# Samples' attention scores over cached keys as TensorE products on transposed keys, and the attention loop moved up behind the top-k with eleven feature tiles in it

## The chip, the cores and the metric

The kernel runs on one core of a Trainium2 chip. The metric is the device time of one execution in microseconds (us). A core has a matrix engine (TensorE, "PE" in the profile, with its weight loads as "PEld"), a vector engine (VectorE, "DVE"), a scalar engine (ScalarE, "ACT"), a general engine (GpSimd, "POOL") and a queue processor (SyncE, "SP"). Each engine works through its own list of instructions in order; they meet only at semaphores.

## What the reference computes

Two decoder layers for one prompt of 512 tokens and eight samples (one new token each). The part that the change touches is the sparse attention of the samples: index scores over 256 cached keys and the new one, the best 64 of them, and softmax attention over those.

```python
def select_keys(qi, wi, ki, qpos, topk):
    s = jnp.einsum('bqhd,bsd->bqhs', qi.astype(jnp.float32), ki.astype(jnp.float32)) * IDX_DIM ** -0.5
    score = jnp.einsum('bqhs,bqh->bqs', jax.nn.relu(s), wi.astype(jnp.float32) * N_IDX_HEADS ** -0.5)
    ...
    _, idx = lax.top_k(score, topk)
...
def dsa_sample(q, k, v, qi, ki, wi, ck, cv, cki, page_table):
    ...
    ki_all = jnp.concatenate([cki[page_table].reshape(n_dec, past, IDX_DIM), ki], axis=1)
    topk = min(TOPK_MAX, (past + t_dec) // 4)
    ...
    return attend(q, kg, vg, valid).reshape(n_dec, t_dec, A_W)
```

There are 4 heads of 64 channels, 8 index heads of 32 channels, and 2 cached pages of 128 keys for each sample. In every layer three other token mixers (a short gated convolution, a convolution of width 31, a state-space scan) and the gated feed-forward part stand beside this.

## The kernel before, in words

A layer is one block of code per engine, run twice by a loop over the layers. All activations are kept with channels on partitions and the 520 tokens (512 of the prompt, 8 of the samples) along the free side.

The stage that matters here runs as follows in each layer.

1. Token products (PE L678 to L697) give queries, keys, values and index queries, with tokens on partitions.
2. DVE adds up the prompt's index scores and takes the best 128 keys of each query in 16 rounds of MAX8 and MATCH_REPLACE (L1550, L1554), then turns the marks into masks (L1558).
3. Under these rounds PE works on *feature tiles*: 18 tiles of 128 output channels, each 48 products (L724). A weight tile is loaded by SP, its upper part cast by ACT (`tile_upper`, L1135), its lower part subtracted by POOL (`tile_lower`, L2034). When a tile's last product is done, ACT first casts the weights of the tile after next and then copies the tile out of PSUM (L1189, inside `feature_out`).
4. After the rounds DVE works out the samples' scores (`for b in range(NS)`, L1567 to L1580): PE spreads a sample's query over all partitions (`spread`, L737 and L738), and DVE multiplies the cached keys by it and adds up over the channels. Between two spreads PE does half a feature tile; four tiles lie there.
5. Then the *attention loop*: 16 steps (`STEPS`: four query blocks by four heads). In step j, PE makes logits (L863), DVE adds the mask and takes the maximum (L1800, L1803), ACT takes the exponential (L1268), DVE divides (L1813), PE transposes the probabilities (L904), ACT copies them out (L1280), and PE mixes the values (L893). PE does `step_products(j)` feature products ahead of the transposes and as many behind them. DVE has one other task in each step (the samples' top-k, softplus, the short convolutions, the samples' states). Five feature tiles lie in the loop.
6. Tiles up to number `LOOP_TILES` alternate between two pairs of PSUM banks; those after it use banks 0 and 1 alone:

```python
        def tile_bank(i):

            return 2 * (i % 2) if i <= LOOP_TILES else 0
...
                                if i >= 2:
                                    pe.wait_ge(feat_ready, i - 1 if i <= LOOP_TILES + 1 else i)
```

so that within the loop a tile's first product waits until ACT has copied the tile before it.

7. Behind the loop PE's first work is `cumulate(0)` (L927), the start of the scan of the prompt.

## Time and profile before

| what | value |
|---|---|
| median of 3 runs | 1547.42 us (1546.89 to 1548.22) |
| profiled execution, its own time | 1550.66 us |
| its span, first to last instruction | 1549.1 us |
| time around the span | 1.56 us |
| mean granted PE clock | 0.96 of full |
| PE busy | 1424.0 us (92%) |
| DVE busy | 844.8 us (55%) |
| ACT busy | 537.3 us (35%) |
| POOL busy | 203.1 us (13%) |

The shares are means over the whole program. The two layers run the same code, one after the other; the first layer's attention stage lies between about 100 and 277 us of the span, and the second layer's is the same some 762 us later. The views by stretch, by engine in order of time and by waits tell what holds this stage up.

### The profile page before, as it was taken

What the parts mean: (1) busy time and instruction counts of PE and PEld (TensorE: products, weight loads), DVE (VectorE), ACT (ScalarE), POOL (GpSimd) and SP (SyncE); (2) the same over time, 40 slices, a digit from 0 to 9 for tenths busy, and PEclk for the clock granted to TensorE, in tenths of its full rate; (3) what the DMA queues carried; (4) which work ended last, traced back from release to release, by engine and by line L of the source; (5) the groups of instructions that cost most, each with busy time, mean ns of one, the idle gap of its engine ahead of it and who ended that gap; (6) DMA issues with size and microseconds to landing.
All of it is one profiled execution on the core that took longest, in us unless ns stands there. A gap on an engine that the chain in (4) does not pass through costs nothing. (4 is left out here: it accounts for less than half of the span.)

```text
span 1549.1 us, 28682 instructions
## 1 busy us (share of the span) xinstructions
PE 1424.0 (92%) x11510; PEld 1319.7 (85%) x11510; DVE 844.8 (55%) x1729; ACT 537.3 (35%) x879; POOL 203.1 (13%) x138
## 2 busy tenths in 40 slices
PE   4999878997999999999769998799989999999995
PEld 4889864897999999999657997558979999999994
DVE  5489998735444444222446898976264443442224
ACT  3443234444322222222344422445342232222222
POOL 1334312020000000000040442311200000000010
PEclk8999988999999999999879998999999999999997
DMA  6443231221333332233055333212313233323221
GB/s 222 133 133 96 80 85 44 97 86 44 94 94 95 88 88 83 76 93 93 9 201 146 104 87 88 81 40 87 96 55 95 84 92 95 92 64 94 84 73 55
DMA packets 222718, 141.20 MB, mean 91 GB/s; under 512 B 13514, under 2 KB 218674, under 8 KB 222102
## 3 DMA queue, kind: packets, MB, share of 16 engines
q1 hardware_dynamic: 220006, 132.57, 29.0%
q0 software_dynamic: 2624, 7.48, 1.3%
q8 instruction: 53, 0.87, 0.2%
q14 instruction: 35, 0.29, 0.1%
HBM read 124.66 MB, written 11.77 MB: 88 GB/s over the span
## 5 line engine op out<-in xcount | busy, mean ns | idle before, releaser
L1861 DVE TENSOR_TENSOR w_lo<-ring,w_hi 128x1024 fp32r<-128x1024 f32 (+2 forms) x164 | 179.3, 1093 | 399.2 <-ACT w_hi L1247 399.2
L623 PE MATMUL PS<-u_hi,w_hi 128*128 128x260 f32 x1600 | 325.5, 285 | 15.4 <-DVE u_lo L1982 11.7
L1247 ACT CAST w_hi<-ring 128x1024 fp32r<-128x1024 f32 (+2 forms) x168 | 158.9, 946 | 473.3 <-PE PS L623 473.3
L623 PE MATMUL PS<-u_hi,w_lo 128*128 128x260 f32 x1600 | 322.4, 283 | 0.0
L623 PE MATMUL PS<-u_lo,w_hi 128*128 128x260 f32 x1408 | 283.8, 283 | 0.0
L623 PEld LDWEIGHTS PS<-u_hi,w_hi 128*128 128x128 f32 x1600 | 246.8, 189 | 18.8 <-issue 13.0
L623 PEld LDWEIGHTS PS<-u_hi,w_lo 128*128 128x128 f32 x1600 | 247.4, 189 | 0.0
L623 PEld LDWEIGHTS PS<-u_lo,w_hi 128*128 128x128 f32 x1408 | 218.3, 189 | 0.0
L623 PE MATMUL PS<-hid_hi,w_hi 128*128 128x260 f32 x704 | 141.8, 283 | 3.6 <-ACTq L1404 3.6
L623 PE MATMUL PS<-hid_hi,w_lo 128*128 128x260 f32 x704 | 141.8, 283 | 0.0
L623 PE MATMUL PS<-hid_lo,w_hi 128*128 128x260 f32 x704 | 141.4, 282 | 0.0
L724 PE MATMUL PS<-u_hi,w_hi 128*128 128x260 f32 x576 | 123.2, 295 | 14.1 <-ACT hid L1189 14.1
L724 PE MATMUL PS<-m_lo,w_hi 128*128 128x260 f32 x576 | 121.7, 291 | 0.0
L2034 POOL TENSOR_TENSOR w_lo<-ring,w_hi 128x1024 fp32r<-128x1024 f32 x36 | 86.3, 2397 | 270.5 <-ACT w_hi L1135 270.4
L724 PE MATMUL PS<-u_hi,w_lo 128*128 128x260 f32 x576 | 121.4, 292 | 0.0
L2115 POOL TENSOR_TENSOR side<-side 128x520 f32<-128x520 f32 x12 | 15.7, 1307 | 762.0 <-ACT u L1415 762.0
L623 PEld LDWEIGHTS PS<-hid_hi,w_hi 128*128 128x128 f32 x704 | 108.4, 188 | 3.9 <-issue 3.9
L724 PEld LDWEIGHTS PS<-u_hi,w_hi 128*128 128x128 f32 x576 | 92.1, 195 | 21.0 <-ACT hid L1189 15.6
L623 PEld LDWEIGHTS PS<-hid_hi,w_lo 128*128 128x128 f32 x704 | 108.4, 188 | 0.0
L623 PEld LDWEIGHTS PS<-hid_lo,w_hi 128*128 128x128 f32 x704 | 108.4, 188 | 0.0
L1999 DVE TENSOR_TENSOR side<-m_lo,PS 128x520 f32<-128x520 f32 x44 | 30.7, 697 | 120.5 <-PE PS L623 120.5
L724 PEld LDWEIGHTS PS<-m_lo,w_hi 128*128 128x128 f32 x576 | 92.3, 194 | 3.2 <-issue 3.2
(346 smaller groups left out, 2192.2 us busy)
## 6 DMA issues: line engine op xcount, KB each, us to landing
ring<-in_ffn_gate SPq DMA_DIRECT2D x44, 512.0 KB, 3.7
ring<-in_ffn_up SPq DMA_DIRECT2D x44, 512.0 KB, 3.7
ring<-in_w_in SPq DMA_DIRECT2D x36, 512.0 KB, 3.6
ring<-in_ffn_down SPq DMA_DIRECT2D x32, 384.0 KB, 3.4
ring<-in_ffn_down SPq DMA_DIRECT2D x32, 320.0 KB, 3.0
ring<-in_w_out SPq DMA_DIRECT2D x16, 512.0 KB, 4.1
x_store<-x SPq DMA_DIRECT2D x2, 2080.0 KB, 15.4
x<-x_store SPq DMA_DIRECT2D x2, 2080.0 KB, 7.8
```

What stands on the lines that cost most here:

```text
L623: ins = pe.matmul(to[:, h, :], w[:, k - base, :], a[k][:, h * HALF:(h + 1) * HALF], start=(begin and w is whi and a is a_hi), stop=(end an ...
L724: last = pe.matmul(bank(tile_bank(i) + h)[:, 0:HALF], w[i % 2][:, k, :], t[:, h * HALF:(h + 1) * HALF], start=(k == 0 and a == 0), stop=(k ...
L1247: act.copy(w_hi[part % 2][:, 0:n, :], raw[part % 4][:, 0:n, :]).then_inc(part_hi, 1)
L1861: dve.tensor_tensor(w_lo[part % 2][:, 0:n, :], raw[part % 4][:, 0:n, :], w_hi[part % 2][:, 0:n, :].bitcast(F32), ALU.subtract).then_inc(pa ...
L1999: dve.tensor_tensor(halves(hid_f[:, c, :]), halves(rstd_all), pair(2 * c + 1), ALU.mult).then_inc(factors_ready, 1)
L2034: pool.tensor_tensor(w_lo[f % 2][:, :, :], raw[(f + 2) % 4], w_hi[f % 2][:, :, :].bitcast(F32), ALU.subtract).then_inc(tile_lo, 1)
L2115: pool.tensor_tensor(squares[:, 0, :], squares[:, 0, :], squares[:, m, :], ALU.add).then_inc(added, 1)
```

## The change

The samples' scores are no longer made by DVE. PE transposes the index keys and the keys of the cache into PSUM (`keys_prepare`, `keys_turn`), ACT copies them to SBUF, and PE multiplies them by the samples' queries, laid out as columns (`index_logits`, `key_products`, `index_scores`). DVE keeps three small preparations (`keys_prepared`, in round 10 of the top-k) and one copy. The attention loop follows the top-k at once. It now has 16 feature products in each half of each of the 16 steps, eleven tiles in all; only five tiles and a third lie ahead of it. The order of the feature slabs is another one, the side tasks of DVE stand in other steps, the samples' states begin in step 11 in place of 13 and use banks 2 and 3, and the convolution of width 31 on PE stands in steps 15 to 17.

The numbers that set the order:

```diff
 
 
-        FEAT_SLABS = [5, 4, 3, 6, 7, 8, 2, 0, 1]
+        FEAT_SLABS = [4, 6, 7, 8, 3, 2, 0, 5, 1]
         N_TOK = 3
 
...
-        SPREAD_FROM = 7
         PER_TILE = 6 * KC
-        PER_SPREAD = PER_TILE // 2
+        PER_PART = PER_TILE // 3
         TAIL_TILES = 2
-        STEP_PRODUCTS = (14, 12, 13, 9, 13, 9, 13, 9, 13, 9, 9)
-        LOOP_TILES = SPREAD_FROM + NS * PER_SPREAD // PER_TILE
-        DENSE_STEPS = 11
+        LOOP_TILES = 5
+        LOOP_FIRST = LOOP_TILES * PER_TILE + PER_PART
         TAIL_PRODUCTS = (8, 20, 20, 12, 36)
         LAST_TILE = len(FEAT_SLABS) * 2 - TAIL_TILES
-        STATES_FROM = 13
+        STATES_FROM = 11
         FIRST_FFN = [(q, [k]) for k in range(5) for q in range(3)] + [(0, [5, 6, 7]), (2, [5, 6, 7]), (1, [5, 6, 7])]
-        TAP_SETS = {12: 2, 13: 3, 14: 3, 15: 3, 16: 3, 17: 2}
+        TAP_SETS = {15: 4, 16: 4, 17: 8}
```

The new functions on PE, and where they stand:

```diff
+                    def keys_prepare():
+
+                        pe.wait_ge(turned_ready, 7)
+                        pe.wait_ge(rope_done, 5)
+                        pe.wait_ge(ki_cache_in, 16 * 2 * NS)
+                        for t in range(NS // 2):
+                            last = pe.transpose(bank(4)[:, t * P:(t + 1) * P],
+                                                ki_cache[:, 4 * t:4 * t + 4, :].rearrange("p i c -> p (i c)"), ident)
+                        last.then_inc(key_pe, 1)
+                        for c in range(2):
+                            pe.transpose(bank(5)[:, c * NS:(c + 1) * NS], tok8[:, c * P:(c + 1) * P], ident[0:NS, 0:NS])
+                            pe.transpose(bank(5)[:, 16 + c * NS:16 + (c + 1) * NS], tok8[:, 3 * W + c * P:3 * W + (c + 1) * P],
+                                         ident[0:NS, 0:NS])
+                        for g in range(4):
+                            last = pe.matmul(bank(5)[32 * g:32 * g + IH, 32:32 + NS], tok8[:, TOK_W - IH:TOK_W], ident[0:NS, 0:NS],
+                                             start=True, stop=True)
+                        last.then_inc(key_prep, 1)
...
+                    def keys_turn(b):
+
+                        if b == 0:
...
+                            pe.wait_ge(keys_kept, b)
+                        for c in range(2):
+                            for pg in range(2):
+                                last = pe.transpose(bank(6 + b % 2)[:, c * W + pg * P:c * W + (pg + 1) * P],
+                                                    k_cache[:, 2 * b + pg, c * P:(c + 1) * P], ident)
+                        last.then_inc(key_pe, 1)
...
+                    def index_logits():
+
+                        pe.wait_ge(queries_kept, 1)
+                        pe.wait_ge(keys_kept, 1 + NS)
+                        for q in range(2):
...
+                        last.then_inc(key_logits, 1)
+
+                    def key_products(q):
+
+                        pe.wait_ge(keys_kept, 1 + 4 * (q + 1))
+                        for c in range(2):
+                            for g in range(4):
+                                b = 4 * q + g
+                                last = pe.matmul(bank(4)[32 * g:32 * g + HEADS, q * W:(q + 1) * W], q_cols[:, c, b, :],
+                                                 k_turned_of[b][:, c * W:(c + 1) * W], start=(c == 0), stop=(c == 1))
+                        if q:
+                            last.then_inc(key_logits, 1)
...
+                    def index_scores():
+
+                        pe.wait_ge(logits_kept, 2)
+                        pe.wait_ge(keys_kept, 1 + NS)
+                        for q in range(2):
+                            last = pe.matmul(bank(6)[0:NS, 0:W], wi_cols[:, q, :], idx_part[:, q * W:(q + 1) * W],
+                                             start=(q == 0), stop=(q == 1))
+                        last.then_inc(dec_pe, 1)
...
-                    feature_products((SPREAD_FROM - 2) * PER_TILE)
-                    pe.wait_ge(turned_ready, 7)
-                    pe.wait_ge(rows_lo_ready, 2)
...
+                        if b in (0, 2, 4, 6):
+                            feature_products(PER_PART)
+                        keys_turn(b)
+                    index_queries()
+                    feature_products(PER_PART)
+                    index_logits()
+                    key_products(0)
+                    feature_products(PER_PART)
+                    key_products(1)
+                    feature_products(LOOP_FIRST - feat_i[0] - PER_PART)
+                    index_scores()
+                    feature_products(PER_PART)
...
+                    def decode_mask():
+
+                        pe.wait_ge(dec_dve, 2)
                         pe.wait_ge(feat_ready, LOOP_TILES + 1)
...
+                        for b in range(NS):
+                            q, r = b // 4, 32 * (b % 4)
+                            last = pe.matmul(bank(2 + q)[r:r + 32, 0:261], ident[0:NS, b:b + 1].broadcast_to([NS, 32]),
+                                             m_row[0:NS, :], start=True, stop=True)
                         last.then_inc(dec_pe, 1)
```

What ACT and DVE do for them, and what DVE no longer does:

```diff
+                    act.copy(ident_r[:, :], ident[0:NS, 0:NS]).then_inc(picks_ready, 1)
+                    act.wait_ge(key_pe, 1)
+                    act.copy(ki_turned, bank(4)).then_inc(keys_kept, 1)
+                    for b in range(NS):
+                        act.wait_ge(key_pe, b + 2)
+                        act.copy(k_turned_of[b], bank(6 + b % 2)).then_inc(keys_kept, 1)
+                        if b == 3:
+                            feature_out(3)
                     feature_out(4)
-                    act.wait_ge(rope_done, 5)
-                    act.copy(rows_hi[:, 0:W], tok8[:, 0:W]).then_inc(rows_hi_ready, 1)
-                    act.copy(rows_hi[:, W:SPREAD_W], tok8[:, 3 * W:TOK_W]).then_inc(rows_hi_ready, 1)
-                    act.copy(ident_r[:, :], ident[0:NS, 0:NS]).then_inc(rows_hi_ready, 1)
+                    act.wait_ge(key_prep, 2)
+                    act.copy(qi_cols.rearrange("p h b -> p (h b)"), bank(5)[:, 64:128]).then_inc(queries_kept, 1)
+                    act.wait_ge(key_logits, 1)
+                    for pg in range(2):
+                        act.activation(idx_part.rearrange("p (q g k) -> p q g k", q=2, g=2)[:, :, pg],
+                                       bank(5 + 2 * pg)[:, 0:W].rearrange("p (q k) -> p q k", q=2), ACT.Relu).then_inc(logits_kept, 1)
+                    act.wait_ge(key_logits, 2)
+                    act.activation(l_row[:, :, 0:W], bank(4).rearrange("p (q k) -> p q k", q=2), ACT.Copy, scale=const("row_used"))\
+                       .then_inc(logits_kept, 1)
                     feature_out(LOOP_TILES)
...
+                    def keys_prepared():
+
+                        dve.wait_ge(key_prep, 1)
+                        step(dve.tensor_tensor(q_cols, bank(5)[:, 0:16].rearrange("p (c b) -> p c b", c=2).unsqueeze(3)
...
+                        settle()
+                        dve.sem_inc(key_dve, 1)
...
-                    dve.wait_ge(k_cache_in, 16 * 2 * NS)
-                    dve.wait_ge(ki_cache_in, 16 * 2 * NS)
-                    for b in range(NS):
-                        qb, ib = bank(4 + 2 * (b % 2)), bank(5 + 2 * (b % 2))
-                        dve.wait_ge(rows_spread, b + 1)
-                        kb = k_cache[:, 2 * b:2 * b + 2, :]
-                        step(dve.tensor_tensor(kb, kb, qb[:, 0:W].unsqueeze(1).broadcast_to([P, 2, W]), ALU.mult))
-                        pi = prod_i.rearrange("p (g h c) -> p g h c", g=2, c=ID)
-                        for pg in range(2):
-                            step(dve.tensor_tensor(pi[:, pg], ki_cache[:, 2 * b + pg, :].unsqueeze(1).broadcast_to([P, IH, ID]),
-                                                   ib[:, 0:W].rearrange("p (h c) -> p h c", c=ID), ALU.mult))
-                        settle()
-                        step(dve.tensor_reduce(past_l[:, :, b, :], kb.rearrange("p g (h c) -> p g h c", c=HD), AX.X, ALU.add))
-                        s16 = sc64[:, 0:16].rearrange("p (g h) -> p g h", g=2)
-                        step(dve.tensor_reduce(s16, pi, AX.X, ALU.add))
-                        settle()
-                        dve.scalar_tensor_tensor(s16, s16, 0.0, ib[:, W + ID:W + ID + IH].unsqueeze(1).broadcast_to([P, 2, IH]),
-                                                 ALU.max, ALU.mult).then_inc(rows_used, 1)
-                        dve.wait_ge(rows_used, b + 1)
-                        step(dve.tensor_reduce(past_s[:, :, b], s16, AX.X, ALU.add))
+                    dve.wait_ge(dec_pe, 1)
+                    step(dve.tensor_copy(s_row[0:NS, 0:W], bank(6)[0:NS, 0:W]))
```

The order of PE's loop and DVE's side tasks:

```diff
-                    pe.wait_ge(rows_used, NS - 1)
+                    pe.wait_ge(logits_kept, 3)
...
+                        if j == 10:
                             turn_state_rows()
-                        if j == 12:
+                        if j == 16:
                             turn_tails()
...
-                        if j == 4:
+                        if j == 3:
                             decode_mask()
-                        if j == 7:
+                        if j == 6:
                             decode_prob_turn()
+                        if j == 8:
+                            decode_mix()
                         if j == 9:
-                            decode_mix()
-                        if j == 10:
                             decode_pick()
...
+                    pe.wait_ge(conv_c_done, 1)
                     cumulate(0)
...
-                            gate_c()
+                            dve.wait_ge(dec_dve, 1)
+                            decode_best(TOPK_SAMPLE // 16)
                         elif j == 2:
-                            decode_scores()
-                            decode_best(TOPK_SAMPLE // 16)
-                        elif j == 3:
                             decode_best(TOPK_SAMPLE // 16)
                             decode_mask()
+                        elif j == 3:
+                            softplus()
                         elif j == 4:
-                            softplus()
+                            decode_logits()
                         elif j == 5:
-                            decode_logits()
+                            decode_probs()
                             conv_d_samples()
...
+                            gate_c()
+                        elif j == 9:
                             conv_d(2)
-                        elif j == 9:
+                        elif j == 10:
+                            state_rows()
                             conv_d(3)
+                        if j == 15:
+                            conv_b(0)
+                        if STATES_FROM <= j < STATES_FROM + NS // 2:
+                            sample_states(j - STATES_FROM)
+                        if j == 11:
                             conv_d(4)
-                        elif j == 10:
+                        elif j == 12:
                             conv_d(5)
                             settle()
                             dve.sem_inc(conv_d_done, 1)
-                        elif j == 11:
-                            state_rows()
+                        elif j == 13:
                             gate_b()
-                        elif j == 12:
-                            conv_b(0)
-                        elif STATES_FROM <= j < STATES_FROM + NS // 2:
-                            sample_states(j - STATES_FROM)
```

TensorE ahead of the loop. In the order before, the last feature products of a tile (L724) are followed by the first sample's spread: the query (`rows_hi`, `rows_lo_q`) and the index query, then half a tile.

```order
L724 MATMUL PS<-u_hi,w_hi_86 128x260 x2
L724 MATMUL PS<-m_lo_70,w_hi_86 128x260 x2
L724 MATMUL PS<-u_hi,w_lo_88 128x260 x2
L737 MATMUL PS<-rows_hi,ident_r 128x256
L738 MATMUL PS<-rows_lo_q,ident_r 128x256
L737 MATMUL PS<-rows_hi,ident_r 128x296
L738 MATMUL PS<-rows_lo_i,ident_r 128x296
```

In the changed order the same place has the last two samples' key transposes (L761, reading `side`), the index queries (L749), a third of a tile (L721), the index logits (L774) and the first half of the key products (L785).

```order
L761 MATMUL PS<-cst,side 128x128 x8
L749 MATMUL PS<-arena,cst 32x64 x4
L721 MATMUL PS<-m_lo_68,w_hi_87 128x260 x2
L721 MATMUL PS<-u_hi,w_lo_89 128x260 x2
L721 MATMUL PS<-u_hi,w_hi_87 128x260 x2
L721 MATMUL PS<-m_lo_69,w_hi_87 128x260 x2
L721 MATMUL PS<-u_hi,w_lo_89 128x260 x2
L721 MATMUL PS<-u_hi,w_hi_87 128x260 x2
L721 MATMUL PS<-m_lo_70,w_hi_87 128x260 x2
L721 MATMUL PS<-u_hi,w_lo_89 128x260 x2
L774 MATMUL PS<-side 8x128 x16
L785 MATMUL PS<-side 4x256 x8
```

The eight spreads are gone; two groups of key work stand where one spread stood, and half tiles have become thirds.

VectorE behind the top-k. Before, the masks (L1558) are followed by a sample's six instructions, eight times over.

```order
L1558 TENSOR_SCALAR arena<-arena 128x512
L1567 TENSOR_TENSOR side<-side,PS 128x512
L1570 TENSOR_TENSOR side<-side,PS 128x256 x2
L1573 TENSOR_REDUCE side<-side 128x2x4
L1575 TENSOR_REDUCE side<-side 128x16
L1577 SCALAR_TENSOR_TENSOR side<-side,PS 128x16
L1580 TENSOR_REDUCE side<-side 128x2
```

Now one copy of eight rows (L1655) stands between the masks (L1651) and the loop's first instruction (L1872).

```order
L1651 TENSOR_SCALAR arena<-arena 128x512
L1655 COPY side<-PS 8x256
L1872 ISA arena,small<-PS,cst 128x128
L1872 ISA small 128x1
L1875 TENSOR_SCALAR small<-small 128x1
```

Forty-eight instructions have gone from this place on DVE.

ScalarE in the loop. Before, the first four exponentials (L1268) of 128 keys and the copies of the probabilities (L1280) have one weight cast (L1135) with its tile's copy (L1189) among them.

```order
L1280 COPY arena<-PS 128x128
L1135 CAST w_hi_87<-ring 128x1024
L1189 ACTIVATE hid<-PS 128x520
L1268 ACTIVATE arena,small<-arena,small 128x128
L1280 COPY arena<-PS 128x128
L1268 ACTIVATE arena,small<-arena,small 128x128
L1280 COPY arena<-PS 128x128
L1135 CAST w_hi_86<-ring 128x1024
L1189 ACTIVATE hid<-PS 128x520
```

Now a cast (L1196) and a tile's copy (L1250) come about every one and a half steps, between the same exponentials (L1344) and copies (L1359); L1284 is the samples' exponential.

```order
L1196 CAST w_hi_87<-ring 128x1024
L1250 ACTIVATE hid<-PS 128x520
L1344 ACTIVATE arena,small<-arena,small 128x256
L1359 COPY arena<-PS 128x128
L1284 ACTIVATE side<-side 128x257 x2
L1344 ACTIVATE arena,small<-arena,small 128x256
L1196 CAST w_hi_86<-ring 128x1024
L1250 ACTIVATE hid<-PS 128x520
L1359 COPY arena<-PS 128x256
```

The cast stands ahead of the copy in each pair, as before; there are eleven pairs in the loop in place of five.

## Rows read from the trace of the kernel before

**Rows 1.** Page: span, and each engine's busy time.

```profile
span 1549.1 us, 28682 instructions
PE 1424.0 (92%) x11510; PEld 1319.7 (85%) x11510; DVE 844.8 (55%) x1729; ACT 537.3 (35%) x879; POOL 203.1 (13%) x138
```

**Rows 2.** Waits, 176 to 276.5 us: who waited for whom; total, times, longest us.

```profile
PE PS L724 <- ACT hid L1189: 7.8, 3, 4.4
...
PE PS L834 <- DVE hid L1739: 3.4, 1, 3.4
...
PE PS L904 <- DVE arena L1813: 3.1, 3, 2.0
...
PE PS L759 <- ACT hid L1189: 1.3, 1, 1.3
...
PE PS L808 <- ACT hid L1189: 1.2, 1, 1.2
```

**Rows 3.** Timeline of PE, 63 to 277 us: start, duration, instructions, idle before.

```profile
63.39 0.71 PE L639 MATMUL PS<-arena 32*128 32x256 f32 x8
...
115.13 1.91 PE L646 MATMUL PS<-cst,arena 128*128 128x128 f32 x16
116.80 0.48 PE L724 MATMUL PS<-u_hi,w_hi 128*128 128x260 f32 x2
117.12 0.41 PE L724 MATMUL PS<-m_lo,w_hi 128*128 128x260 f32 x2
...
145.81 0.38 PE L737 MATMUL PS<-rows_hi,ident_r 8*128 8x256 f32 x1
...
149.58 0.38 PE L737 MATMUL PS<-rows_hi,ident_r 8*128 8x256 f32 x1
...
176.01 0.49 PE L863 MATMUL PS<-arena 64*128 64x128 f32 x4
...
212.26 0.80 PE L724 MATMUL PS<-u_hi,w_hi 128*128 128x260 f32 x2 [4.38 <-ACT hid L1189]
...
232.01 1.07 PE L787 MATMUL PS<-x,side 128*32 128x256 f32 x16
...
276.54 2.05 PE L927 MATMUL PS<-cst,dt_tiles 128*128 128x128 f32 x16
```

**Rows 4.** Timeline of DVE, 147 to 218 us.

```profile
147.31 2.93 DVE L1558 TENSOR_SCALAR arena<-arena 128x256 f32<-128x256 f32 x3
150.28 0.69 DVE L1567 TENSOR_TENSOR side<-side,PS 128x512 f32<-128x512 f32 x1
...
153.26 0.68 DVE L1567 TENSOR_TENSOR side<-side,PS 128x512 f32<-128x512 f32 x1
...
175.94 0.17 DVE L1580 TENSOR_REDUCE side<-side 128x2 f32<-128x16 f32 x1
...
211.78 4.50 DVE L1719 SCALAR_TENSOR_TENSOR side<-hid,par,side 128x511 f32<-128x511 f32 x3
...
217.76 2.32 DVE L1719 SCALAR_TENSOR_TENSOR side<-hid,par,side 128x511 f32<-128x511 f32 x3
```

**Rows 5.** Timeline of POOL, 211 to 247 us.

```profile
211.79 2.37 POOL L2034 TENSOR_TENSOR w_lo<-ring,w_hi 128x1024 fp32r<-128x1024 f32 x1 [10.76 <-ACT w_hi L1135]
...
242.55 3.65 POOL L2073 TENSOR_TENSOR side<-cst,tap_col 128x2048 f32<-128x2048 f32 x1
```

**Rows 6.** Timeline of ACT, 197 to 199 us.

```profile
197.51 1.05 ACT L1135 CAST w_hi<-ring 128x1024 fp32r<-128x1024 f32 x1 [3.18 <-PE PS L724]
198.46 0.60 ACT L1189 ACTIVATE hid<-PS 128x520 f32<-128x520 f32 x1
```

**Rows 7.** Stretches of 10 us: busy of PE, PEld, DVE, ACT, POOL; granted PE clock; DMA.

```profile
190.00:200.00 10.00, 6.29 (x36) 4.84 (x36) 9.35 (x35) 2.80 (x7) 1.36 (x1) 0.83 0.48 122
...
210.00:220.00 10.00, 7.74 (x45) 7.27 (x47) 9.61 (x19) 3.08 (x8) 2.37 (x1) 0.66 0.37 107
...
240.00:250.00 10.00, 6.56 (x36) 3.38 (x36) 9.68 (x20) 2.37 (x6) 6.17 (x4) 0.58 0.46 157
```

249 lines of the change are left out of this document (126 added, 123 removed).

## The prediction

> **What bounds the kernel now.** I read the page first. PE is busy for 92% of the span and DVE for 55% [rows 1], so over the whole program a shorter DVE list is worth nothing by itself; it counts only where PE waits for it. So next came the stage of the change. In the first layer the top-k ends at 150.24 (147.31 plus 2.93), the eight samples' scores run from 150.28 to 176.11, and the attention loop begins at once [rows 4]. PE's own list shows that it is not idle under these scores: it starts a sample's spread at 145.81 and 149.58, with half a feature tile between, and its first product of the loop stands at 176.01 [rows 3]. Both engines come to the loop at the same moment. Of the loop, from 176.01 to `cumulate(0)` at 276.54, the view of waits gives PE's idle time: 7.8 + 3.4 + 3.1 + 1.3 + 1.2 = 16.8 us [rows 2]. Only 3.1 us of it is the wait for probabilities from DVE. Most, 7.8 us, is PE waiting for ACT to empty the one PSUM pair (the largest 4.38 us at 212.26 [rows 3]). The stretches then show a second loss: the granted clock is 0.83, 0.66 and 0.58 in three slices of 10 us, each with PE under 8 us busy [rows 7]. Busy time times the missing clock is 6.29 x 0.17 + 7.74 x 0.34 + 6.56 x 0.42 = 6.5 us. So in each layer some 23 us of PE time between 115 and 277 could be had, and everything else there is PE's work. That is the ceiling of the gain, 2 x 23 = 46 us, not the 2 x 25.9 us that DVE loses.
>
> **The change part by part, for one layer.**
>
> *DVE's scores.* 150.28 to 176.11 is 25.8 us, 2.98 a sample (150.28 to 153.26 [rows 4]) plus small waits near the end. In their place stand three small preparations, about 0.8 us (I take the price of three small instructions of 0.17 us with their starts and the wait between them), and a copy of about 0.4. DVE therefore starts the loop at 150.2 + 1.2 = 151.5, or 25 us sooner. The cost of this to PE is nothing directly.
>
> *PE ahead of the loop.* The work removed is eight spreads. 145.81 to 149.58 is 3.77 us for one spread and 24 feature products. Five tiles, 240 products, take from 116.80 to 145.81, or 0.121 us each, so 24 cost 2.90 and a spread 0.87; eight are 7.0 us [rows 3]. Added are 36 transposes of 128x128; sixteen such took 115.13 to 116.80, 0.104 each, so 3.8 us [rows 3]. Eight tiny products and the four of the index queries I bound between 0 and 0.104 each and take 1.6 us with their starts. The sixteen index logits: four products of 256 columns in four row groups took 0.71 us [rows 3]; with half the columns, four groups of four are between 4 x 0.36 and half of that, so 1.0. The sixteen key products have the shape of the samples' mix (sixteen records, that is eight products, about 1.05 us [rows 3]), so 2.1. The two index scores are 0.9 (between the mix's pace, 0.3, and two logits, 1.1). Sum 9.4, net +2.4.
>
> *PE in the loop.* The mask is eight products for one (+0.5), the probabilities' turn six transposes for three small ones (+0.4), and the turn of the scores goes (-0.4). Feature products are cut into about nine more pieces; the first pair of a piece takes 0.32 us (116.80 to 117.12) where a pair costs 0.24 [rows 3], so +0.9 with rounding up. Work in sum: +2.4 + 0.5 + 0.9 = +3.8 us. Feature products themselves only move: 16 tiles before, 16 now.
>
> *When PE reaches the loop.* 116.80 + 160 products (19.3) + 9.4 + waits. ACT copies the transposed keys out under the feature products; only before the index logits must PE wait, for a weight cast, a tile's copy (0.95 + 0.60 [rows 6]) and the copy of the queries, 2.1 us in all. So PE is there at about 149, before DVE at 151.5. It fills the gap with the 48 products that stand ahead of its first wait (5.8 us).
>
> *The waits in the loop.* Eleven tiles in one PSUM pair make nine boundaries at which PE must wait for ACT. ACT casts first and copies then: 197.51 to 199.06 is 1.55 us, and with the product's own tail and the semaphores a bare boundary costs PE 1.9 [rows 6]. I walked the sixteen steps with each engine in its own order and prices as in these rows. The boundaries then cost 1.7, 0.9, 0.7, 1.2, 1.6, 1.8 (here it is the samples' output that is waited for), 0, 1.9 and 2.5: 12.3 us. Where the mask's products or transposes stand between two tiles, they hide a part of ACT's 1.55. The waits for probabilities come to 4.6, nearly all in steps 13 to 15, where DVE has two tasks in a step and ACT the SiLU of the convolution with its table loads. With 2.3 ahead of the loop this is 19.2 us, against 16.8 before: +2.4. The same walk in the order of before reaches `cumulate(0)` at 275.0, where the trace has 276.54; that is how far I trust it.
>
> *The clock.* With PE never idle for more than 2.5 us I expect less of the low clock, not none: the last steps look like 190 to 200 us of now [rows 7]. Of the 6.5 us I leave 2.8: -3.7. Both ends are possible, 0 and 6.5, and they enter the range.
>
> *DVE against POOL.* At 211.78 a group of three instructions took 4.50 us where the same group took 2.32 at 217.76; POOL lowered a weight tile from 211.79 on for 2.37 us [rows 4, 5]. Such a collision costs DVE up to 2.2 us. Under MAX8 and MATCH_REPLACE the lowerings cost it nothing. Now five more of them fall into the loop: +11 us for DVE. Its loop took 176.1 to about 276, so it would take at most 100 + 11 + 1 = 112 us, from 151.5 to 263.5. That is still ahead of PE, so the term is nothing on PE's path but the late waits counted above. The Trainium skill ("SBUF — State Buffer", Who interferes with whom) says that a DVE instruction with two SBUF inputs is fully blocked by a GpSimd one that reads SBUF; by it eleven lowerings of 2.37 and the tap weights' 3.65 [rows 5] could stop DVE for 29.7 us in place of the 15 or so of before, and its end would be near 267, the sum for PE unchanged.
>
> *Tail, loads.* Behind the loop PE's order is the same, and so are the products in it. The caches' rows are wanted some 30 us sooner than now, behind the first feature products, but their loads keep their place far ahead in the queues' lists, SP's weight loads keep their order, and POOL's state load now waits for the samples' mix in step 8 and is needed in step 11, some 18 us later. I cost these at nothing; if the state load were late, PE's spreads would stop in step 11.
>
> **Sum.** Work +3.8, waits +2.4, clock -3.7: +2.5 us a layer, +5 us for two. Against the profiled execution's own 1550.66 this is 1555.7; that execution was 3.2 us above the median, so against the median it is 1547.4 + 5 = 1552.
>
> **The rivals.**
>
> *A. The loop closes up (faster).* The ledger's waits are the soft term. If transposes and logits hide ACT's 1.55 us at most of the nine boundaries, as they do at the one that costs nothing, waits fall from 19.2 to 11, and with PE then hardly idle the clock stays at its full level: +3.8 - 5.8 - 6.5 = -8.5 a layer, 1530. For it speaks that DVE is 25 us ahead; against it, that ACT casts before it copies, and that five boundaries have the next tile's product almost directly behind. It decides from waits under 16.5 us a layer on with the clock as I have it. 0.27, for anything from 1525 to 1544.
>
> *B. The clock takes it back.* PE is now on the path at every moment, so a slice at 0.6 costs its full 4 us, where before it cost partly slack. If the three slices of [rows 7] come again, the clock term is 0: +6.2 a layer and 1560. For it: nine idle gaps of 1 to 2.5 us; against it, that the slices of now follow gaps of 3.4 and 4.4. 0.15.
>
> *C. DVE becomes the bound.* If collisions cost DVE the 29.7 us, it ends at 151.5 + 100 + 14.7 + 1 = 267, 10 us ahead of PE. Only if each of the sixteen steps adds a little over 1 us more in which DVE and PE wait for each other in turn, 18 us, does it end near 285; then the layer loses 8: 1547.4 + 16 = 1564. The price of DVE's list speaks against it; it decides from an end of DVE behind 277 on. 0.06.
>
> *D. My forecast, and around it no effect:* what DVE gives up was hidden behind PE. 0.52, and in this case 1546 to 1558.
>
> **Chances and range.** A measurement of this kernel tells about 0.2% (3.1 us) from no change, so faster means below 1544.3 and slower above 1550.5. Case A gives 0.25 faster and 0.02 same. Case D gives 0.23 same, 0.27 slower and 0.02 faster. B and C are slower, 0.21. Faster 0.27, same 0.25, slower 0.48. The work term is open by 2 us a layer, the waits by 3 in either direction, the clock from -2.8 to +3.7; taken together that is 5.5 a layer or 11 in all: 1541 to 1563. For eight in ten this leaves out most of A below 1541 and a little of C.
>
> **What the profile after would show.** L1872 first at about 151.5, PE's first logits near 149, `cumulate(0)` between 276 and 281 in the first layer. PE's waits in the loop are mostly for ACT's tile copy, some nine of 1 to 2 us; DVE idle for some 35 us of the loop. The clock is below 0.9 in one slice rather than three. The prediction is wrong if `cumulate(0)` stands before 273, which would mean that the boundaries were hidden, or after 283; and wrong in its reason if the largest wait of PE in the loop is for DVE.

## The result, and the profile after

| | changed kernel | before |
|---|---|---|
| median of 20 runs | 1550.6 us (1548.58 to 1555.91) | 1548.94 us (1545.3 to 1552.29) |
| ratio | 1.0018, interval 1.0009 to 1.0026 | |
| profiled execution, its own time | 1550.77 us | 1550.66 us |

The change costs 1.4 to 4.0 us by this interval, most likely 2.8; a later measurement of the same two kernels gave 1.0017 (1.0006 to 1.0027). The forecast was 4.6 us above the median of before, with 1541 to 1563 as its range. In the two profiled executions the difference is 0.1 us, so the traces don't show the 2.8 us as one place. They show how the parts of the sum came out.

About half of the cost sits in a few executions. Of the 32 executions of the changed kernel in the two measurements, nine took 1553.84 to 1555.91 us, longer than any of the 102 of the kernel before that are on record beside these runs (1552.75 at most); the other 23 average 1550.3 us. The mean granted clock of the nine is 0.959, that of the 23 is 0.962; this is worth some 4 us of PE's 1428, most of the 4.7 by which they are longer. Neither trace of the changed kernel (1550.77 and 1550.88 us) is of one of the nine, so what lowers the clock in them stays open.

The page of the changed kernel, against [rows 1]: DVE has lost 50.8 us of work and PE has gained 3.5.

```profile
span 1549.2 us, 29026 instructions
PE 1427.5 (92%) x11720; PEld 1325.7 (86%) x11720; DVE 794.0 (51%) x1623; ACT 550.9 (36%) x907; POOL 200.9 (13%) x134
```

The timeline of PE in the first layer, against [rows 3]: start, duration, instructions, idle before.

```profile
118.67 0.66 PE L733 MATMUL PS<-cst,side 128*128 128x128 f32 x4
...
119.75 0.51 PE L721 MATMUL PS<-u_hi,w_lo 128*128 128x260 f32 x2
...
121.77 1.03 PE L761 MATMUL PS<-cst,side 128*128 128x128 f32 x8
122.56 0.48 PE L721 MATMUL PS<-m_lo,w_hi 128*128 128x260 f32 x2
...
135.37 0.66 PE L774 MATMUL PS<-side 32*8 32x128 f32 x32 [1.79 <-ACT side L1269]
135.96 1.05 PE L785 MATMUL PS<-side 128*4 128x256 f32 x16
136.94 0.51 PE L721 MATMUL PS<-u_hi,w_hi 128*128 128x260 f32 x2
...
144.05 1.03 PE L795 MATMUL PS<-arena,side 128*8 128x256 f32 x4
...
147.13 0.49 PE L927 MATMUL PS<-arena 64*128 64x128 f32 x4
...
153.41 0.27 PE L964 MATMUL PS<-cst,arena 128*128 128x128 f32 x1
...
159.84 0.50 PE L721 MATMUL PS<-u_hi,w_hi 128*128 128x260 f32 x2 [1.58 <-ACT hid L1250]
...
239.17 1.12 PE L964 MATMUL PS<-cst,arena 128*128 128x128 f32 x4 [5.04 <-DVE arena L1885]
...
274.74 2.05 PE L987 MATMUL PS<-cst,dt_tiles 128*128 128x128 f32 x16
```

The loop begins at 147.13 and not at 176.01, and the new work ahead of it can be read from the gaps: the preparations take 1.2 us (118.67 to 119.75, and a tenth ahead), a group of eight transposes 0.79 and 0.08 more for the first pair behind it, index logits with the first half of the key products 1.57. `cumulate(0)` stands at 274.74, 1.8 us before that of [rows 3].

The view of waits, PE, 100 to 300 us, against [rows 2] (L1250 is ACT's copy of a tile, L1885 DVE's division of the probabilities, L1269 the copy of the index queries, L1290 that of the samples' output):

```profile
PE PS L721 <- ACT hid L1250: 8.2, 7, 1.7
PE PS L964 <- DVE arena L1885: 6.3, 2, 5.0
PE PS L774 <- ACT side L1269: 1.8, 1, 1.8
PE PS L872 <- ACT ya L1290: 1.6, 1, 1.6
```

The waits for ACT are many and short, as forecast. But the longest single wait is for DVE. The timelines of DVE and POOL at that place, with the first instruction of DVE's loop (L1872) ahead of them:

```profile
148.86 0.27 DVE L1872 CUSTOM_DVE_ANT_0 arena<-PS,cst 128x128 f32<-128x128 f32 x1
...
209.92 0.17 DVE L1822 COPY small<-PS 128x16 f32<-128x16 f32 x1 [4.78 <-PE PS L879]
...
229.72 7.65 DVE L1791 SCALAR_TENSOR_TENSOR side<-hid,par,side 128x511 f32<-128x511 f32 x3
```

```profile
229.55 2.39 POOL L2108 TENSOR_TENSOR w_lo<-ring,w_hi 128x1024 fp32r<-128x1024 f32 x1 [10.03 <-ACT w_hi L1196]
231.90 4.14 POOL L2147 TENSOR_TENSOR side<-cst,tap_col 128x2048 f32<-128x2048 f32 x1
```

The group of three that takes 2.32 us alone [rows 4] takes 7.65 under the lowering of a weight tile (L2108) and the making of the tap weights of the width-31 convolution (L2147), which POOL does back to back. PE's transposes of step 12 wait 5.04 us for it. Twenty microseconds earlier DVE stood idle for 4.78 us.

Stretches of 10 us of the changed kernel, with the columns of [rows 7]:

```profile
190.00:200.00 10.00, 8.53 (x92) 6.15 (x91) 8.83 (x21) 2.65 (x6) 2.39 (x1) 1.00 0.20 52
...
210.00:220.00 10.00, 10.00 (x78) 8.30 (x78) 7.61 (x21) 3.71 (x8) 2.35 (x1) 1.00 0.53 133
...
230.00:240.00 10.00, 4.93 (x36) 3.98 (x36) 9.59 (x12) 0.81 (x2) 6.04 (x2) 0.91 0.52 136
240.00:250.00 10.00, 9.33 (x46) 6.77 (x44) 6.85 (x30) 3.94 (x6) 1.16 (x1) 0.74 0.01 2
...
310.00:320.00 10.00, 10.00 (x73) 9.90 (x72) 4.99 (x7) 2.78 (x4) 2.17 (x2) 0.83 0.21 66
```

The low clock of 190 and 210 is gone. That of 240 has stayed, behind the 5.04 us. And there is a new one at 310, which costs 10.00 x 0.17 = 1.7 us: it stands outside the stage, in products that the change doesn't touch, and gives back the lead of 1.8 us that the loop had won. The second layer has such a slice too (0.83 at 1070).

### The profile page after: what moved, and what is told of

The parts are those of the page before. It is cut to its first block and busy times, and to the rows that moved or that the text cites. A ratio compares the mean times of both kernels' runs of the same rounds, so it can differ in the third digit from the quotient of the medians.

```text
span 1549.2 us, 29026 instructions
## 1 busy us (share of the span) xinstructions
PE 1427.5 (92%) x11720; PEld 1325.7 (86%) x11720; DVE 794.0 (51%) x1623; ACT 550.9 (36%) x907; POOL 200.9 (13%) x134
## 5 line engine op out<-in xcount | busy, mean ns | idle before, releaser
L620 PE MATMUL PS<-u_hi,w_hi 128*128 128x260 f32 x1600 | 325.9, 285 | 15.1 <-DVE u_lo L2056 11.4
L620 PEld LDWEIGHTS PS<-u_hi,w_hi 128*128 128x128 f32 x1600 | 247.1, 189 | 19.1 <-issue 13.5
L620 PEld LDWEIGHTS PS<-u_hi,w_lo 128*128 128x128 f32 x1600 | 248.0, 190 | 0.0
L721 PE MATMUL PS<-u_hi,w_hi 128*128 128x260 f32 x576 | 121.1, 292 | 16.4 <-ACT hid L1250 16.4
L2108 POOL TENSOR_TENSOR w_lo<-ring,w_hi 128x1024 fp32r<-128x1024 f32 x36 | 86.0, 2389 | 296.3 <-ACT w_hi L1196 296.2
L721 PE MATMUL PS<-u_hi,w_lo 128*128 128x260 f32 x576 | 120.7, 292 | 0.0
L721 PE MATMUL PS<-m_lo,w_hi 128*128 128x260 f32 x576 | 119.4, 289 | 0.0
L721 PEld LDWEIGHTS PS<-u_hi,w_hi 128*128 128x128 f32 x576 | 91.1, 193 | 24.5 <-ACT hid L1250 20.6
L721 PEld LDWEIGHTS PS<-u_hi,w_lo 128*128 128x128 f32 x576 | 90.7, 193 | 5.6 <-issue 5.0
```

What stands on the lines that cost most here:

```text
L620: ins = pe.matmul(to[:, h, :], w[:, k - base, :], a[k][:, h * HALF:(h + 1) * HALF], start=(begin and w is whi and a is a_hi), stop=(end an ...
L721: last = pe.matmul(bank(tile_bank(i) + h)[:, 0:HALF], w[i % 2][:, k, :], t[:, h * HALF:(h + 1) * HALF], start=(k == 0 and a == 0), stop=(k ...
L2108: pool.tensor_tensor(w_lo[f % 2][:, :, :], raw[(f + 2) % 4], w_hi[f % 2][:, :, :].bitcast(F32), ALU.subtract).then_inc(tile_lo, 1)
```

## The experiments

Twelve runs were made: each of the two kernels once more, three edits of the kernel before and seven of the changed one. "Stage" is the time from the first feature product behind the token products (103.33 in the first layer of the changed kernel) to `cumulate(0)`, in the first and the second layer. "Low clock" is busy time of PE times the missing clock, summed over slices of 10 us, 100 to 280 and 860 to 1040, for both layers together. Where a text below says "theory 1", PE's own list and the clock set the time; "theory 2" is that DVE, slowed by POOL, sets the pace of the last steps.

**The two kernels again.** The changed kernel:

> The changed kernel itself, for a second trace and a second ratio. Theory 1 (PE's own list sets the time: what the loop wins, the clock takes back at a place that lies by chance) expects 1.001 to 1.003 of the time before, cumulate(0) near 275 again, and low-clock stretches that stand elsewhere or cost another amount than in the first trace. Theory 2 (DVE, slowed by POOL, sets the pace of the last steps) expects the waits of PE for the probabilities to be the same in both traces, 5 us and 1.3 us in the first layer.

The kernel before:

> The kernel before, for a second trace. If the clock's place is chance, its low stretches differ from the first trace, by up to some 3 us in sum, and the engines' order of events does not. If it is bound to the order of the work, both traces show 0.83, 0.66 and 0.58 in the same slices between 190 and 250.

The ratio was 1.0017 (1.0006 to 1.0027). The four traces:

| trace | stages | PE's waits in them | low clock |
|---|---|---|---|
| before | 172.95, 172.47 | 17.1, 16.6 | 15.2 |
| before, again | 174.05, 172.54 | 18.7, 16.6 | 15.0 |
| changed | 171.41, 170.51 | 17.9, 15.2 | 7.4 |
| changed, again | 172.64, 173.62 | 16.3, 15.3 | 13.5 |

(The 17.1 holds one wait of 0.3 us that [rows 2] leaves out.) The order comes back, and so do the waits for ACT, to a tenth but for one pass: the first layer of the changed kernel has 8.2 us of waits for tiles in the one trace and 9.2 in the other. What moves most is the clock. The second trace of before has it partly in other slices than [rows 7] (1.00 at 190, 0.95 at 200, 0.71 at 210, 0.67 at 240), with nearly the same sum over the stage, and one at 310 that the first trace lacks:

```profile
190.00:200.00 10.00, 5.10 (x37) 3.99 (x37) 9.38 (x33) 3.13 (x8) 2.38 (x1) 1.00 0.40 92
200.00:210.00 10.00, 6.32 (x45) 4.66 (x44) 8.90 (x56) 2.83 (x10) 0.00 (x0) 0.95 0.43 100
210.00:220.00 10.00, 8.85 (x54) 7.84 (x55) 9.38 (x18) 2.44 (x6) 2.37 (x1) 0.71 0.34 100
...
310.00:320.00 10.00, 9.05 (x63) 9.05 (x64) 5.47 (x9) 4.43 (x6) 3.26 (x2) 0.83 0.22 67
```

The changed kernel's second trace has no low clock at 310 (1.00) but one of 0.83 at 210, where PE was busy throughout and the first trace has 1.00. So the order of the work alone does not fix the place or the depth, though both traces of before have a low clock at 210 and at 240, and a reading of one trace is good to some 3 us a layer. Theory 2's claim failed as I put it: the 5.04 us wait was not in the second trace (2.3 at most, three waits of 3.7 in sum). There the same two POOL instructions met DVE's list a little elsewhere: the group of three took 4.33 us, and a division of the probabilities behind it 2.58 where it takes 0.49 alone (first layer of the second trace).

```profile
231.77 4.33 DVE L1791 SCALAR_TENSOR_TENSOR side<-hid,par,side 128x511 f32<-128x511 f32 x3
...
237.36 2.58 DVE L1885 TENSOR_SCALAR arena<-arena,small 128x512 f32<-128x512 f32 x1
```

The second layers of both traces look like this one (4.32 and 2.59, 4.33 and 2.59), so the 7.65 us are one pass of four; the waits for it in the other three are 2.3 to 2.5 us.

**Is DVE's release worth anything alone?**

```diff
-step(dve.tensor_tensor(kb, kb, qb[:, 0:W].unsqueeze(1).broadcast_to([P, 2, W]), ALU.mult))
-for pg in range(2):
+for pg in range(0):
     step(dve.tensor_tensor(pi[:, pg], ki_cache[:, 2 * b + pg, :] ..., ALU.mult))
 ...
-step(dve.tensor_reduce(past_l[:, :, b, :], kb.rearrange(...), AX.X, ALU.add))
+step(dve.tensor_copy(past_l[:, :, b, :], kb[:, :, 0:HEADS]))
-step(dve.tensor_reduce(s16, pi, AX.X, ALU.add))
+step(dve.tensor_copy(s16, ki_cache[:, 2 * b:2 * b + 2, 0:IH]))
```

> The kernel before, with the three large products and the large sum of each sample's scores left out on DVE (small copies stand in for the sums, so the samples' attention is not computed); PE's spreads and everything else stay. It does alone what the change does for DVE. Theory 1 (PE's own list brings it to the loop at 176, whatever DVE does): no effect, 0.999 to 1.001 of the time before, first logits again near 176. Rival (DVE's 25.8 us were on the path): 3 us or more a layer, under 0.996.

Measured: 1.0007 (0.9997 to 1.0017). The kernel leaves the products and sums of the scores out, and DVE is busy for 806.4 us where it was 844.8, 19 us a layer less. DVE now waits for each spread in turn (L738), and PE comes to the loop at 175.75, where it had come at 176.01 before:

```profile
153.92 0.17 DVE L1572 COPY side<-side 128x8 f32<-128x8 f32 x1 [2.39 <-PE PS L738]
157.69 0.17 DVE L1572 COPY side<-side 128x8 f32<-128x8 f32 x1 [3.12 <-PE PS L738]
```

That shows the first point of the prediction: a shorter DVE list is worth nothing here by itself.

**And PE's share of the scores?** The edit of DVE stays, and on PE a spread becomes two short products:

```diff
-pe.matmul(to, pick, part, start=True, stop=False)
-last = pe.matmul(to, pick, lo, start=False, stop=True)
+last = pe.matmul(to[:, to.shape[-1] - 16:], pick, part[:, part.shape[-1] - 16:], start=True, stop=True)
```

> As no_dve_scores, and each sample's spread on PE is one short product in place of four (some 0.2 us in place of 0.87). Theory 1: PE reaches the loop some 5.4 us sooner, 10.7 us for two layers, and the clock may take back half: 0.993 to 0.997. Rival (the loop's own waits absorb an earlier start): 0.998 to 1.

Measured: 0.995 (0.9935 to 0.9965), 7.7 us, by four executions. The loop began only 3.3 us sooner than in [rows 3] (172.72), not 5.4, since two short products still stood for a spread. By the ratio all of that arrived, 2 x 3.3 us; in the trace, which is of the longest of the four, `cumulate(0)` stands 2.1 us sooner (274.4). PE's list is the bound here.

**PE's list ahead of the loop, in the changed kernel.** In each function the transposes and products of the keys are cut to one (the same is done in `keys_prepare` and `key_products`), so that the samples' attention is left out:

```diff
 def keys_turn(b):
-    for c in range(2):
-        for pg in range(2):
+    for c in range(1):
+        for pg in range(1):
 ...
 def index_logits():
-    for q in range(2):
-        for pg in range(2):
-            for g in range(4):
+    for q in range(1):
+        for pg in range(1):
+            for g in range(1):
 ...
```

> The changed kernel with most of the key transposes and score products left out on PE (one transpose of four for a sample, one index logit of sixteen, two key products of sixteen), so that the samples' attention is not computed. PE's list ahead of the loop is 5 to 6 us shorter. Theory 1 with DVE's top-k as the next bound: PE is at the loop near 141.5, but the first probabilities are there only at about 152.1, where PE took them at 153.41; so it wins 1.3 us a layer and waits for the rest: 0.998 to 0.9995 of the changed kernel, and a wait of some 4 us for DVE at the first transposes. Rival (PE's list is the only bound): 11 us, 0.993.

Measured: 1.0004 (0.9994 to 1.0013) of the time before, so 0.9986 of the changed kernel. PE is at the loop at 144.90, and then:

```profile
144.90 0.49 PE L927 MATMUL PS<-arena 64*128 64x128 f32 x4
152.47 0.33 PE L964 MATMUL PS<-cst,arena 128*128 128x128 f32 x1 [1.12 <-DVE arena L1885]
```

It had taken the first probabilities at 153.41 without a wait; now it takes them at 152.47 with one. Of 2.2 us of lead 0.9 arrive. (That the wait is 1.1 and not 4 is because PE came at 144.9, not at 141.5; the text put the removed work at 5 to 6 us. A part of the rest is a slice at 0.83 of the clock, 130 to 140, with PE busy for 8.21 us: 1.4 us that neither trace of the changed kernel has there.) By this run cheaper key work would bring this kernel some 2 us (the interval allows up to 4), and DVE's top-k is the next bound.

**The ends of tiles.** In `feature_out`, ACT's copy of the finished tile goes ahead of the cast of the next weights:

```diff
-                            if i + 2 < len(feat_tiles):
-                                tile_upper(i + 2)
                             act.wait_ge(feat_summed, i + 1)
 ...
                             act.activation(halves(feat[:, 2 * s + c, :]), pair(tile_bank(i) // 2), func).then_inc(feat_ready, 1)
+                            if i + 2 < len(feat_tiles):
+                                tile_upper(i + 2)
```

> The changed kernel, but ACT copies a finished tile out of PSUM first and casts the next weights then. Theory 1: each of the waits of PE for ACT (8.2 us in seven waits in the first layer's loop, 1.6 ahead of the samples' state rows, 1.8 ahead of the index logits) falls by the 0.95 us of the cast, or to nothing where it is less: 7.6 us a layer, 12 to 15 in all, 0.990 to 0.992 of the changed kernel. Theory 2: DVE cannot follow in the last steps, PE's wait for the probabilities grows by what the tiles give, and less than half of it, under 7 us, arrives.

Measured: 0.9973 (0.996 to 0.9986) of the time before, 0.9955 of the changed kernel: 7 us, half of what I expected. The waits did what the rows said (PE, 100 to 285 us):

```profile
PE PS L721 <- ACT hid L1248: 3.3, 4, 1.5
PE PS L964 <- DVE arena L1885: 2.1, 2, 1.8
PE PS L774 <- ACT side L1269: 1.7, 1, 1.7
PE PS L872 <- ACT ya L1290: 1.5, 1, 1.5
```

Seven waits of 8.2 us are four of 3.3, and DVE's didn't grow. (The waits of 1.8 and 1.6 stayed, and I should not have counted them: the cast and the tile's copy both stand ahead of the copy that PE waits for there, in either order.) PE's waits in the two stages are some 15 us less in sum (17.3 against 33.1 and 31.6). In the trace much of that is taken back by the clock, with 42 us of low clock over the whole kernel against 32 and 33 in the two traces without the edit. Over all twelve executions the mean granted clock is 0.959 against 0.962, which is worth 3.4 us of PE's 1430; what becomes of the other 4 to 5 us the runs don't show. The first layer's slices in the trace:

```profile
220.00:230.00 10.00, 7.55 (x36) 6.59 (x35) 9.42 (x29) 2.83 (x5) 0.22 (x1) 0.65 0.41 100
230.00:240.00 10.00, 10.00 (x66) 8.16 (x65) 7.64 (x27) 1.68 (x4) 6.02 (x2) 0.84 0.33 99
240.00:250.00 10.00, 8.34 (x57) 7.29 (x58) 8.54 (x31) 8.71 (x14) 2.39 (x1) 0.83 0.11 33
```

The same edit in the kernel before:

> The kernel before with the copy of a finished tile ahead of the cast of the next weights on ACT. PE has five waits for the copy in a loop (10.3 us), each should fall by 0.95: 4.7 us a layer, of which copy_first_after lets me expect that half arrives, 5 us in all, 0.995 to 0.998. Rival (the ends of tiles were not what held PE in this order, DVE was): 0.999 to 1.

Measured: 1.0003 (0.9994 to 1.0012), as the rival had it. The waits for ACT fell from 10.3 to 5.3 us, as computed, but those for the probabilities came to 6.0, where the two traces of before have 3.1 and 5.0:

```profile
PE PS L904 <- DVE arena L1813: 6.0, 6, 2.0
PE PS L724 <- ACT hid L1187: 4.8, 3, 3.4
PE PS L834 <- DVE hid L1739: 3.6, 1, 3.6
```

In sum 15.2 us of waits are left of 17.1 and 18.7. In the second layer nothing is won: the waits for the probabilities are 7.4 us there, where both traces of before have 2.9, and the sum stays at 16.6. Over the whole trace PE's waits are 116.7 us against 120.6 and 121.2. The clock takes that back: the low clock over the whole kernel is 38 us against 34 and 36, and the mean granted clock is 0.957 over the eleven executions, where that of 82 executions of the kernel before is 0.961. Read with the run above, this says what the change has done: in the old order DVE stands close behind ACT among those that PE waits for, and takes over when ACT gets faster; in the new order DVE is far enough ahead that a faster ACT pays.

**The tap weights.** The call that makes the tap weights on POOL (L2147) stands behind the lowering of tile 12, where POOL waits for the samples' picks anyway:

```diff
                         if f == 12:
                             pool.wait_ge(dec_pe, 4)
                             for i in range(2):
                                 pool.dma_start(ssm[...], ...).then_inc(ssm_half[i], 16)
-                        if f == 15:
                             tap_weights()
```

> The changed kernel with POOL's tap weights (4.14 us) ahead of the lowering of tile 13, where DVE is idle, and not behind that of tile 15, where both together made three DVE instructions take 7.65 us for 2.32. Theory 2: the wait of 5.04 us goes in the first layer and that of 2.3 in the second, 7 us in all, 0.9955 of the changed kernel. Theory 1: PE's wait for probabilities goes too, but some of it turns up as a longer wait for ACT or as low clock behind it: between 0 and 4 us, 0.9975 to 1.

Measured: 0.9977 (0.9966 to 0.9988) of the time before, 0.9959 of the changed kernel. It was 6 us, near theory 2's 7.

```profile
206.66 3.69 POOL L2147 TENSOR_TENSOR side<-cst,tap_col 128x2048 f32<-128x2048 f32 x1 [4.24 <-PE PS L861]
```

It now lies in DVE's idle time (205 to 210), and takes 3.69 us where it took 4.14; DVE's group at 230.53 takes 4.51 us, from the lowering alone. PE's waits for the probabilities are 2.1 and 1.5 us in the two layers; without the edit they are 6.3 and 3.6 in the one trace, 3.7 and 3.7 in the other. That is 5 us less in two layers. Over the whole trace PE's waits are 113.5 us against 117.3 and 117.2, since one wait for a tile grew by 1 us, and the mean granted clock over the nine executions is 0.964 against 0.962, worth some 3 us. So the 6 us are the shorter waits and a higher clock together.

**The scores on PE without the new loop.**

```diff
-        LOOP_TILES = 5
+        LOOP_TILES = 11
-            return PER_PART if 0 <= j < len(STEPS) else 0
+            return 7 if 0 <= j < len(STEPS) else 0
-                    feature_products(LOOP_FIRST - feat_i[0] - PER_PART)
+                    feature_products(2 * PER_PART)
                     index_scores()
-                    feature_products(PER_PART)
+                    feature_products(LOOP_FIRST - feat_i[0])
 ...
-                        if f == 12:
+                        if f == 14:
```

> The changed kernel's scores on PE, but with the old share of feature tiles in the loop: eleven and a third tiles ahead of it and 7 products in each half of a step (POOL's load of the samples' states moves behind tile 14). It does the one half of the change without the other. By PE's list, the loop begins at 147.1 + 34.8 (288 products of 0.121) = 182, against 176 before, and then takes some 98.5 to 100: cumulate(0) at 280 to 282, 3 to 5 us a layer later than before, 1.004 to 1.007 of the time before. Rival (where the tiles stand is worth nothing, DVE's release and PE's work are all): 1.0017, as the whole change.

Measured: 1.0191 (1.0176 to 1.0207), three to five times what I expected. The start was right (182.35), the loop was not: it took 108.7 us, to 291.06. PE's waits from 181 to 292:

```profile
PE PS L964 <- DVE arena L1885: 13.3, 8, 2.5
PE PS L721 <- ACT hid L1250: 7.2, 3, 3.2
PE PS L872 <- ACT ya L1290: 0.4, 1, 0.4
```

With 14 products in a step, PE is through before DVE and ACT have the next probabilities, eight times; one slice stands at 0.50 of the clock, and the low clock from 190 to 280 comes to 13.4 us. Over the whole trace the waits are 133 us against 117, and the low clock 45 against 32 and 33: together 28 of the 30 us. In the changed order the convolution of width 31 no longer helps to fill the steps 12 to 14 either, and the old order had 18 to 28 feature products in each of its first eleven steps and none behind them, where this run has 14 in all sixteen; I didn't separate either from the number of tiles. What is shown is that in the changed order of tasks the loop needs the eleven tiles: with fewer the scores on PE cost 30 us, with them 3.

**The edits together.**

> The changed kernel with the copy ahead of the cast and with the tap weights moved early. The two gave 6 us each. If they act at different waits and the clock takes nothing more, 12 us: 0.994 of the time before. If the clock takes back again what the shorter waits give (42 us of low clock in copy_first_after against 32), 8 to 9 us: 0.996.

Measured: 0.9925 (0.9905 to 0.9945), 11.6 us less than before. They add up: 2.8 above, less 7 and 6, would be 10.3 less, well within the interval of 8.5 to 14.7. Of PE's waits 8.3 and 11.4 us are left in the two stages.

The queries' copy ahead of tile 3's, on ACT:

```diff
-                    feature_out(4)
                     act.wait_ge(key_prep, 2)
                     act.copy(qi_cols..., bank(5)[:, 64:128]).then_inc(queries_kept, 1)
+                    feature_out(4)
```

> The changed kernel, with ACT's copy of the index queries ahead of the cast and the copy of tile 3, so that PE doesn't wait 1.8 us ahead of the index logits. If PE's list is the bound, 3.6 us for two layers: 0.9977 of the changed kernel. But the light_keys_after run gave only some 2 us for a list that was 2.5 us a layer shorter at the loop's start, and the first probabilities come from a DVE that leaves its top-k at 148.5: then PE wins at most the 1.3 us between 152.1 and 153.41 in a layer, 0.9985, and waits for DVE or ACT in the first steps for the rest.

Measured: 1.0003 (0.9992 to 1.0014) of the time before, 0.9985 of the changed kernel. The 1.8 us wait is gone, the loop begins at 144.80, and the first transposes wait again:

```profile
151.61 0.33 PE L964 MATMUL PS<-cst,arena 128*128 128x128 f32 x1 [0.37 <-DVE arena L1885]
```

> All three edits: copy ahead of the cast, tap weights early, queries first. both_after stands at 0.9925 of the time before; with the queries first, 1.5 to 3.5 us less: 0.990 to 0.9925. If the first steps are bound by DVE, no more than both_after: 0.9925.

Measured: 0.9928 (0.9915 to 0.9941), median 1537.99 us. No more than both_after, within the intervals. In the second layer DVE is now what PE waits for most (PE, 800 to 1045 us), as in both_after (6.4 us there); in the first layer the two are level, 3.2 us for DVE and 3.3 for the tiles:

```profile
PE PS L964 <- DVE arena L1885: 6.9, 5, 2.7
PE PS L721 <- ACT hid L1248: 1.8, 3, 0.7
```

## Why the prediction came out as it did

The direction and the first reason hold: DVE's time was hidden, PE's list decides, and the whole is a little slower. The size was too large by 2 us only, and that closeness is luck: the waits were put some 3.5 us a layer too high, the work about 1.3 too high, and the clock was given 3.5 that it did not give over many executions. Term by term, for one layer, with means over the four stages of each kernel:

- *Work ahead of the loop*: 9.4 forecast; the gaps in PE's timeline give 9.3 (1.2, four times 0.87, 0.5, 1.7, 1.2 and 1.2). The wait for the queries was 1.8 for 2.1 (2.3 where the text adds up the waits). PE's arrival, "about 149", was a slip: its own terms give 147.6, and 147.13 was measured. DVE began at 148.86 and not 151.5: the three preparations stand in the rounds and delayed the masks by 0.4 us only (the masks stand at 147.48, behind a top-k that began 0.3 us sooner), and the masks took 1.01 us where they took 2.93 under a lowering (147.31 in [rows 4], with POOL's lowering from 147.09 on).
- *Work as a whole*: +3.8 forecast. The stage became 1.0 us shorter (173.0 to 172.05), with waits 1.1 and low clock 2.4 less; that leaves +2.5. The parts in the loop were priced about 1 us too high.
- *Waits*: +2.4 forecast (19.2 against 16.8), measured -1.1 (16.2 against 17.2). This term failed. Nine boundaries were walked at 12.3 us with the state rows; eight waits of 9.8 came in the first trace. And both ends of the difference moved: the second trace of before has 18.7 in the first layer where the first has 17.1, so the base was itself good to 2 us only. The largest wait was for DVE in three of the four passes (5.04, 2.3 and 2.5 us; in the fourth it is 2.3 against 2.5 for a tile), which the text had named as the mark of a wrong reason. In sum ACT stays ahead, 11.6 to 12.6 us a layer against 3.6 to 6.3. And much of DVE's lateness was POOL's doing (with the tap weights moved, the waits for it fell from 4.3 us a layer on average to 1.8), not the length of its list.
- *"The term is nothing on PE's path but the late waits counted above"*, of DVE against POOL: too light. The tap weights and a lowering back to back cost one group 5.3 us in one pass, and in the three others 2.0 us in the group and 2.1 in the division behind it. Moving them was worth 6 us in two layers, the largest single thing next to the ends of tiles. That DVE has much idle time in sum doesn't help where it is behind for one step.
- *Clock*: -3.7 forecast, measured -2.4 in the stage of these traces, but +0.5 behind it (0.83 at 310 and 1070 in one trace of two, against one in four stretches before). And the traces flatter it: their mean granted clock is 0.960 twice before and 0.962 twice after, while over all executions with a clock on record it is 0.9613 (82 of the kernel before) and 0.9616 (32 of the changed one). That difference is worth 0.2 us a layer. So this term failed as well: it is rival B's clock, nothing won, beside waits that were lower than B's.
- *Rival A* (faster, the boundaries hidden) needed 11 us of waits. Two small edits brought the waits down to 8.3 and 11.4, and the kernel to 0.9925, 1537 us and not the 1530 of the text, whose clock did not come: the case was real in its waits, but not this kernel's.
- *Rival C* (DVE the bound) did not come near: DVE's last instruction of the loop ends at 259.8 in the first layer of the first trace, 3.7 us ahead of the forecast's 263.5 and 15 ahead of `cumulate(0)`.
- `cumulate(0)` came at 274.74 and 276.44, the first a little ahead of the 276 to 281 that were named, neither ahead of 273.

By the two measured ratios the change costs 2.6 to 2.8 us, and by the stages of the traces it should have won 2. The clock closes most of this gap: both traces of before are of executions longer than their median (by 1.7 and 2.3 us) and of a lower clock than the mean, those of the changed kernel are of a slightly higher one, and the two deviations, 0.0013 and 0.0004 of some 1425 us, make 2.4 us, to about 1 us, since a clock is on record to three places. The rest of the traces' gain is lost outside the stage, 1.7 us on average, in parts that differ by up to 3 us between two traces of one kernel. As an estimate for one layer over all executions, work +2.5, waits -1.1 and clock -0.2 make +1.2, and the ratios say +1.3 to +1.4. The work in it is what the traces of the stage leave over, and the waits are from two traces of each kernel, so this holds to about 1 us; and why nine executions of 32 are some 5 us longer than the others is not among its terms.

## What to carry to other kernels

Work that is taken from an engine off the path is worth nothing until the order is changed so that the bound engine can use the room; here the first half alone gave 1.0007 or 1.0191, and the room paid only with two further edits. When an order packs one engine tightly, look next at who releases it and in what order (a copy that someone waits for goes ahead of a cast that nobody waits for yet), and for long instructions on a neighbour that can be put where the victim is idle. A saving of waits on the matrix engine should not be counted at full value before it is measured, as long as the granted clock moves too: here 15 us of shorter waits gave 7, some 4 in the old order gave nothing, and 4 with the tap weights gave 6. And a trace is one execution: its clock should be set beside the mean of all before its parts are added up.

## What was not expected of the hardware

- The granted clock of a slice differs between two executions of one kernel (1.00 and 0.83 at 210 for the changed kernel, with PE busy for 10.00 us of 10 in both), while the low clock over the whole of the kernel before was 34 and 36 us.
- With shorter waits the clock was lower in copy_first_after (42 us of low clock for 32 and 33, with PE's waits some 15 us less; 0.959 over the executions) and in copy_first_before (0.957 for 0.961), but higher in taps_early_after (0.964 for 0.962). In three_edits_after the low clock was 33 us, with waits for tiles of 3.3 and 1.8 us. So shorter waits alone do not settle which way it goes, and no fixed share can be given.
- Two POOL instructions back to back (2.39 and 4.14 us) stretched three DVE instructions from 2.32 to 7.65 us in one pass, more than twice what one lowering adds (4.51 in taps_early_after). In the other three passes the same three took 4.32 or 4.33 us, and the next division 2.58 or 2.59 where it takes 0.49 alone.
